# The columns of a large matmul in another order, and the activations 64 bytes further on

## The reference, cut to what matters

```python
p = rmsnorm(x, norm_mix) @ w_in
x = x + concatenate([y_a, y_b, y_c]) @ w_out
up = dwconv3(rmsnorm(x, norm_ffn) @ ffn_w_up); gate, val = split(up)
x = x + (silu(gate) * val) @ ffn_w_down
proj = rms_norm(x, norm_g) @ w_in_2; kv = rms_norm(mem, mem_norm_g) @ w_mem_kv
merged = sigmoid(ga) * (ya @ w_up_a) + sigmoid(gb) * (yb @ w_up_b) + sigmoid(gc) * (yc @ w_up_c)
return x + merged @ w_o
```

## Time and profile before

| | |
|---|---|
| median of three runs | 2315.16 us (2314.85 to 2325.08) |
| span of the profiled execution | 2314.3 us |
| TensorE, matmuls | 2298.7 us busy, 99%, 22128 instructions |
| TensorE, weight loads | 2264.9 us busy, 98%, 22128 instructions |
| VectorE | 1529.2 us busy, 66% |
| ScalarE | 1114.5 us busy, 48% |
| read from HBM | 396.81 MB, 172 GB/s over the span |

### The profile page before, as it was taken

The page is one execution under the profiler, slowest core; times in us unless marked ns, Lnnn a source line. Parts: engine busy times, 40 slices in busy tenths (PEclk is TensorE's granted clock), DMA queues, the critical chain, the costliest instruction groups (busy, mean ns, idle before and its releaser), DMA issues.

```text
span 2314.3 us, 54222 instructions
## 1 busy us (share of the span) xinstructions
PE 2298.7 (99%) x22128; PEld 2264.9 (98%) x22128; DVE 1529.2 (66%) x2109; ACT 1114.5 (48%) x1513; POOL 12.8 (1%) x27
## 2 busy tenths in 40 slices
PE   8999999999999999999999999999999999999999
PEld 7999999999999999999999999999999999999999
DVE  7668767666545666678786677777767555555554
ACT  6443445555434555444644455555546444444442
POOL 0000000000000000000000000000000000000000
PEclk9999999999999999999999999999999999999999
DMA  7553556555555555655554444343434455556554
GB/s 272 168 178 120 181 181 195 187 190 186 187 190 186 188 190 186 223 186 179 195 177 147 132 141 132 129 148 126 135 125 139 163 186 189 190 185 189 190 186 162
DMA packets 110533, 401.44 MB, mean 173 GB/s; under 512 B 12538, under 2 KB 12565, under 8 KB 110240
## 3 DMA queue, kind: packets, MB, share of 16 engines
q1 hardware_dynamic: 108288, 390.91, 51.6%
q0 software_dynamic: 2080, 8.06, 1.1%
HBM read 396.81 MB, written 2.10 MB: 172 GB/s over the span
## 4 chain that ended last, share of the span: by engine, by line
PE 97%; DVE 2%; DMA 0%; issue 0%; ACT 0%; SPq 0%; DVEq 0%; ACTq 0%
PE bank L473 96%; DVE w_lo L1650 1%; DMA raw<-in_units 0%; DVE x L1699 0%; ACT w_hi L1102 0%; PE bank L908 0%; DVE prod L1696 0%; DVE acc L1696 0%; DVE scaled_in L1696 0%; PE bank L834 0%; ACT x L1185 0%; SPq L1067 0%; SPq L1072 0%; DVE fh L1703 0%; PE bank L1009 0%
## 5 line engine op out<-in xcount | busy, mean ns | idle before, releaser
L1650 DVE TENSOR_TENSOR w_lo<-raw,w_hi 128x1024 fp32r<-128x1024 f32 x736 | 894.6, 1223 | 637.4 <-ACT w_hi L1102 632.3
L1102 ACT ACTIVATE w_hi<-raw 128x1024 fp32r<-128x1024 f32 x736 | 778.6, 1059 | 855.2 <-PE bank L473 846.3
L473 PE MATMUL bank<-h_hi,w_hi 128*128 128x256 f32 x4016 | 1134.7, 283 | 8.9 <-DVE h_lo L1699 8.9
L473 PE MATMUL bank<-h_lo,w_hi 128*128 128x256 f32 x4016 | 1121.9, 279 | 0.0
L473 PE MATMUL bank<-h_hi,w_lo 128*128 128x256 f32 x4016 | 1121.2, 279 | 0.0
L473 PEld LDWEIGHTS bank<-h_hi,w_hi 128*128 128x128 f32 x4016 | 755.5, 188 | 15.0 <-DVE h_lo L1699 8.9
L473 PEld LDWEIGHTS bank<-h_lo,w_hi 128*128 128x128 f32 x4016 | 755.7, 188 | 1.6
L473 PEld LDWEIGHTS bank<-h_hi,w_lo 128*128 128x128 f32 x4016 | 755.4, 188 | 0.0
L473 PE MATMUL bank<-m_hi,w_hi 128*128 128x256 f32 x704 | 196.7, 279 | 0.0
L473 PE MATMUL bank<-m_lo,w_hi 128*128 128x256 f32 x704 | 196.5, 279 | 0.0
L473 PE MATMUL bank<-m_hi,w_lo 128*128 128x256 f32 x704 | 196.5, 279 | 0.0
(11 more groups left out here) (434 smaller groups left out, 2734.8 us busy)
## 6 DMA issues: line engine op xcount, KB each, us to landing
raw<-in_units SPq DMA_DIRECT2D x736, 512.0 KB, 3.6
memx<-in_memT POOLq DMA_DIRECT2D x4, 512.0 KB, 8.1
out_y<-obuf SPq DMA_DIRECT2D x8, 256.0 KB, 4.4
x<-in_xT SPq DMA_DIRECT2D x3, 512.0 KB, 9.0
bias_t<-in_bias POOLq DMA_DIRECT2D x8, 192.0 KB, 2.6
dft<-in_dft POOLq DMA_DIRECT2D x1, 1024.0 KB, 10.9
decay<-in_decay POOLq DMA_DIRECT2D x1, 768.0 KB, 7.7
x<-in_xT SPq DMA_DIRECT2D x2, 256.0 KB, 4.5
```

What stands on the lines that cost most here:

```text
L473: return pe.matmul(out, lhsT, rhs, start=start, stop=stop, skip_group_check=True)
L1102: return act.activation(out, in_, ACT.Copy, scale=scale)
L1650: dve.tensor_tensor(w_lo[slot][:, :, :], raw[slot][:, :, :], w_hi[slot][:, :, :].bitcast(F32), ALU.subtract).then_inc(split_done, 1)
```

## The change

The 256 columns of each large matmul are no longer gone through in order. A new helper `turned` sees the row as two halves of 128 columns, each as 32 groups of four. It goes through the groups from the last to the first, and at each takes the group of the first half and then that of the second: columns 124 to 127, 252 to 255, 120 to 123, 248 to 251, and so on down to 0 to 3, 128 to 131. Moving operand and output get the same order, so that the same sums end in the same places. It is applied in `unit`, in the down loop and in `part`. The matmuls of 512 columns, the norm sums, the small products and the weight loads keep their order. Second, `h_at` is 64 bytes further on, and with it `h_hi`, `h_lo` and the whole shared area.

```diff
+LINE = 4
...
-        h_at = (nc.sbuf_base + 31) // 32 * 32
+        h_at = (nc.sbuf_base + 31) // 32 * 32 + 64
...
+        def turned(ap2d):
+
+            return ap2d.rearrange("p (q s e) -> p s q e", q=2, e=LINE)[:, ::-1, :, :]
...
-                        rh, rl = hi[:, k0 + kk, :], lo[:, k0 + kk, :]
-                        mm(o[:, t, :], wh, rh, first and kk == 0 and t == 0, False)
-                        mm(o[:, t, :], wh, rl, False, False)
-                        m = mm(o[:, t, :], wl, rh, False, last and kk == UK - 1 and t == tiles - 1)
+                        out = turned(o[:, t, :])
+                        rh, rl = turned(hi[:, k0 + kk, :]), turned(lo[:, k0 + kk, :])
+                        mm(out, wh, rh, first and kk == 0 and t == 0, False)
+                        mm(out, wh, rl, False, False)
+                        m = mm(out, wl, rh, False, last and kk == UK - 1 and t == tiles - 1)
...
-                                o = p2(pair[t // 2])[:, t % 2, :]
+                                o = turned(p2(pair[t // 2])[:, t % 2, :])
...
-                                rh, rl = m_hi[:, 2 * u + kk, :], m_lo[:, 2 * u + kk, :]
+                                rh, rl = turned(m_hi[:, 2 * u + kk, :]), turned(m_lo[:, 2 * u + kk, :])
```

More of the change, by code:

```diff
@@ L754, in part @@
                         wl = w_lo[slot][:, kk, t * P:(t + 1) * P]
[L755 to L758, removed]
+                        out = turned(o[:, t, :])
+                        rh, rl = turned(hi[:, (k % 4) * UK + kk, :]), turned(lo[:, (k % 4) * UK + kk, :])
+                        mm(out, wh, rh, k % 4 == 0 and kk == 0 and t == 0, False)
+                        mm(out, wh, rl, False, False)
+                        m = mm(out, wl, rh, False, k % 4 == 3 and kk == 3 and t == 1)
                 if half != 0:
```

## The result

The changed kernel takes 2467.69 us (median of four runs, 2467.51 to 2468.74) against 2316.03 before: ratio 1.064, 95% interval 1.0618 to 1.0662. That is 152 us more. The forecast was 2191 us.

The account below looks back on a forecast made before the run. TensorE's pace through 17616 large matmuls at 116.7 ns was taken as the bound. From 2315.2 us, 130 us of stall go and 6 us of lost cover come: 2191 us, own range 2160 to 2215, 8 in 10 2160 to 2400.

Parts of the forecast that it names:

- What bounds the kernel: Whole kernel: TensorE's pace through 17616 float32r matmuls of 256 columns at 116.7 ns, 2056 us, 89% of the span.
- The stall of 7.4 ns: Each 256-column float32r matmul: excess time in its 116.7 ns, expected to go entirely, 7.4 x 17616 = 130 us.
- the floor of 109.3: Each turned 256-column matmul: 109.3 ns start to start with the stall gone, a unit shrinking from 2.80 to 2.62 us.
- The same everywhere, for different tensors (so different addresses): Large matmuls in all windows: 116.7 ns whatever the tensor, address or VectorE and ScalarE load.
- The 64 bytes at nothing: Shift of `h_at`: changes the distance to the weight load by four groups, costed by itself at nothing for the other engines.
- the two readers meet and part: Plain order: the matmul runs over its row at twice the weight load's pace, hitting it in some of the groups.
- part (1): The new column order in the large matmuls: no instruction added, only the sequence against the weight load changes; 130 us less.
- the lower end: Price of the new order: all of the stall goes, 130 us at 2.6 ns an instruction, 153 us if per pass.
- rival 2: Large matmuls slower: wrong fixed distance, or the two halves collide with each other; 2445 or 2790 us; chance 0.23.
- light end: Milder size of rival 2: 32 pairs add 7.4 ns a matmul to the stall that stays, +130 us, 2445.
- the weight load to read from its last column down: Condition in part (1): if so, matmul and load keep a fixed distance, collisions either gone or permanent; no size given.
- The 512 columns: Unturned 512-column matmuls: 230 ns each against 215.9, 14 ns of stall, taken as evidence that the stream alone stalls.

Follow-up runs that it names:

- four parts: TensorE alone, single matmuls: groups of four columns taken in turn from four parts of the row instead of two halves, neighbours 256 bytes apart; 134.0 to 138.0 ns.

## Why the prediction was wrong

**What bounds the kernel** was right. The distance between starts in the 17616 large matmuls is what moved, and it accounts for 153 of 152 us. Nothing else became late, the clock stayed at its upper level, and the plain float32 matmuls have room.

**The stall of 7.4 ns** can be had only in part: with groups of 16, 3.4 ns of it go. No order or distance tried went below 113.3 ns, so the floor of 109.3 worked out from the earlier trace rows was not seen, and since 128 columns already take 110.6 ns, it may not be the floor of a matmul that has a weight load beside it.

**"The same everywhere, for different tensors (so different addresses)"** was a misreading of the earlier trace rows. The tensors have different addresses, but `place` puts nearly all of them at whole kilobytes from one `arena_at`, so modulo 256 bytes every moving row stood at the same distance from the weights. The rows could not show a dependence on the address, and I took that for its absence. (The load varied more than I wrote: in the stretch from 430 us VectorE is busy 70% and ScalarE 53%, which only helps that part of the argument.)

**The 64 bytes at nothing** was wrong. In plain order they are 54 us (116.7 to 120.0 ns). I had argued that the two readers meet and part in plain order whatever the distance. In the new order, where I let the distance decide everything, it decides nothing between 32 and 96 bytes: 2466.72 and 2467.69 us.

**The step that failed** is the choice in part (1): "the matmul stays two groups on one place and advances at the pace of the weight load", read as a way to keep clear of the weight load, and priced near the lower end, all of the stall gone. The sentence describes the cost. With groups of four, pairs 512 bytes apart took 8.7 ns a matmul more than plain order in the full kernel and 8.5 with TensorE alone, where the forecast had 7.4 ns less; groups 64 bytes apart took less than plain order. That the two groups get in each other's way in the storage is the reading that fits; no run looks inside. It is rival 2, which had that mechanism and a time of 2445 for its light end; it got 0.23, against 0.40 for the forecast. Its price, 0.23 ns a pair, measured 8.7 / 32 = 0.27. That this came so close is luck: the price was the old stall taken once more, without a reason, and with four parts a pair costs (136.8 - 116.7) / 48 = 0.42. What could have turned the choice: the forecast needed the weight load to read from its last column down, for which no row stood, and needed neighbours on one place to be free, for which there was none either. Rival 2 needed only the second to be false.

**The 512 columns** The earlier trace rows spoke, I wrote, for a stall of the stream alone. That was too strong: the pair shown is at the low end of the 32 in that trace, whose mean is 236 ns, and with TensorE alone they take 226.7 to 234.6 ns by distance, so their stall runs from 11 to 19 ns. Only the row was shifted there, so how much of it is the weights' is not shown.

The Trainium skill ("SBUF — State Buffer", A bandwidth-pool intuition that's wrong, in the table) gives TensorE two independent read ports, for the moving operand and the weights. If that meant that the two can't delay each other, the times could not depend on where the weights lie; they do, 116.7 against 120.0 ns. The Trainium skill's "Advanced Engine Details and Errata" (PSUM Cachelines) says that any non-contiguous pattern slows matmuls significantly, by which the pieces written should have cost: they cost 0.2 us. Its other sentence, that every two consecutive elements should be contiguous, agrees with that.

**Open.** What repeats at 256 bytes; why 16 bytes of shift count even when both sides move, and why they decide so much with groups of eight; why 32 columns of weights stall a matmul no less than 128; why some distances have two rhythms. No kernel without weight loads was run, so how much of any stall is the stream's own is open.

## What to carry to other kernels

Where TensorE is the bound and streams float32r, take the start-to-start distance of one matmul against what its columns need, and if there is a stall, try where the moving rows lie against the weights modulo 256 bytes: 64 bytes were worth 54 us of 2316 here, for no instruction. Run the candidate several times, since some distances have two rhythms. Don't let consecutive groups of 16 bytes lie 128, 256 or 512 bytes apart. And before reading "the same for all tensors" as "independent of the address", look whether the allocator gives them all the same low bits.

## What the runs showed of the hardware that I had not expected

The stall of a 256-column float32r matmul runs from 113.3 to 120.0 ns in plain order with the distance to the weights' place, with a period of 256 bytes, and with all other engines idle it is the same as in the full kernel at 32 and 96 bytes. At 192 bytes the same instructions run at 113.5 or at 117.8 ns a matmul. In groups of eight, a change of 16 bytes in the distance moves a matmul between 126.5 and 113.4 ns. A float32r matmul of 128 columns takes 110.6 ns, one of 256 no less than 113.3. The order of the writes into PSUM, in groups of four, made no difference above 1.4 us in the whole kernel.
